# Attention scores of two mixers as stacked float32r products, a short run of ones at the beginning, and single waits for the embedding's banks

## What is computed

```
# sink mixer: 16 query heads, 4 key heads of width 64, window 128
scores = einsum('bnqkgd,bnskd->bnkgqs', q, kb) * 64 ** -0.5
scores = where(band, scores, -inf); m = max(scores, sink); e = exp(scores - m)
probs = e / (sum(e) + exp(sink - m)); out = probs @ v
# sparse mixer, 8 query heads, 2 key heads of width 64; N_CMP = 15 compressed keys
s_c = q @ k_cmp.T * scale ; s_s = q @ k_selected.T * scale ; s_w = q @ k_window.T * scale
o = g0 * softmax(s_c) @ v_cmp + g1 * softmax(s_s) @ v_slc + g2 * softmax(s_w) @ v_win
```

## Time and profile before

| | |
|---|---|
| median of 3 runs | 1202.47 us |
| the profiled execution | 1201.95 us, of which its span (first to last instruction) 1200.2 us |
| TensorE matmul (PE) busy | 1185.6 us, 99% |
| VectorE (DVE) busy | 747.8 us, 62% |
| ScalarE (ACT) busy | 619.5 us, 52% |
| GpSimd (POOL) busy | 43.9 us, 4% |
| DMA | 210.78 MB, 176 GB/s over the span |

### The profile page before, as it was taken

The page is one execution under the profiler, slowest core; times in us unless marked ns, Lnnn a source line. Parts: engine busy times, 40 slices in busy tenths (PEclk is TensorE's granted clock), DMA queues, the critical chain, the costliest instruction groups (busy, mean ns, idle before and its releaser), DMA issues.

```text
span 1200.2 us, 16205 instructions
## 1 busy us (share of the span) xinstructions
PE 1185.6 (99%) x6405; PEld 1006.8 (84%) x6405; DVE 747.8 (62%) x991; ACT 619.5 (52%) x925; POOL 43.9 (4%) x64
## 2 busy tenths in 40 slices
PE   9999999999999999999999999999999999999998
PEld 7888899898787889999888888888878788888887
DVE  6769645556865774554697455447986465554447
ACT  5464544344465544444456434436886674444445
POOL 2000000000000000000000000001111010000001
PEclk9999999999999999999999999999999999999999
DMA  8656554654653366556545565554651336555550
GB/s 285 216 186 209 193 191 163 209 196 154 228 177 114 114 210 197 190 177 204 181 146 183 198 206 179 180 172 144 191 167 69 114 124 210 198 188 175 176 175 36
DMA packets 119963, 210.78 MB, mean 176 GB/s; under 512 B 8320, under 2 KB 67024, under 8 KB 119888
## 3 DMA queue, kind: packets, MB, share of 16 engines
q1 hardware_dynamic: 119344, 209.35, 52.5%
q10 hardware_dynamic: 544, 0.40, 0.1%
HBM read 208.68 MB, written 1.05 MB: 175 GB/s over the span
## 4 chain that ended last, share of the span: by engine, by line
PE 91%; DVE 4%; ACT 2%; DMA 1%; issue 1%; POOL 0%; SPq 0%; ACTq 0%; DVEq 0%; POOLq 0%
PE psum L341 23%; PE psum L343 23%; PE psum L342 23%; PE psum L349 4%; PE psum L350 4%; PE psum L355 4%; PE psum L1430 2%; PE psum L1398 2%; DMA ring<-in_a_w_in 1%; DVE wl L324 1%; PE psum L1417 1%; PE psum L852 1%; PE psum L540 1%; PE psum L1404 0%; DVE arena L3607 0%
## 5 line engine op out<-in xcount | busy, mean ns | idle before, releaser
L293 DVE TENSOR_TENSOR wl<-ring,wh 128x2048 fp32r<-128x2048 f32 x131 | 300.0, 2292 | 263.1 <-ACT wh L284 263.0
L284 ACT ACTIVATE wh<-ring 128x2048 fp32r<-128x2048 f32 x131 | 250.6, 1915 | 215.2 <-PE psum L343 215.2
L341 PE MATMUL psum<-wh,xT_high 128*128 128x512 f32 (+4 forms) x592 | 231.4, 391 | 0.2 <-DVE wl L324 0.2
L343 PE MATMUL psum<-wh,xT_low 128*128 128x512 f32 (+4 forms) x592 | 225.1, 380 | 0.0
L342 PE MATMUL psum<-wl,xT_high 128*128 128x512 f32 (+4 forms) x592 | 224.4, 379 | 0.0
L341 PE MATMUL psum<-wh,hidT_high 128*128 128x512 f32 (+2 forms) x472 | 178.8, 380 | 0.2
L342 PE MATMUL psum<-wl,hidT_high 128*128 128x512 f32 (+2 forms) x472 | 178.0, 379 | 0.0
L343 PE MATMUL psum<-wh,hidT_low 128*128 128x512 f32 (+2 forms) x472 | 177.9, 378 | 0.0
L341 PEld LDWEIGHTS psum<-wh,xT_high 128*128 128x128 f32 x592 | 111.3, 188 | 21.6 <-issue 2.0
L343 PEld LDWEIGHTS psum<-wh,xT_low 128*128 128x128 f32 x592 | 111.2, 188 | 21.1
L324 DVE TENSOR_TENSOR wl<-ring,wh 128x1024 fp32r<-128x1024 f32 (+4 forms) x101 | 121.2, 1218 | 11.5 <-ACT wh L314 10.8
(11 more groups left out here) (323 smaller groups left out, 1479.6 us busy)
## 6 DMA issues: line engine op xcount, KB each, us to landing
ring<-in_mlp_w_up SPq DMA_DIRECT2D x32, 1024.0 KB, 5.5
ring<-in_mlp_w_down SPq DMA_DIRECT2D x32, 1024.0 KB, 5.0
ring<-in_ffn_wg SPq DMA_DIRECT2D x44, 512.0 KB, 4.0
ring<-in_ffn_wu SPq DMA_DIRECT2D x44, 512.0 KB, 5.0
ring<-in_ffn_wd SPq DMA_DIRECT2D x22, 1024.0 KB, 5.0
ring<-in_ple_w_gate SPq DMA_DIRECT2D x12, 1024.0 KB, 5.0
ring<-in_w_in SPq DMA_DIRECT2D x10, 1024.0 KB, 5.2
ring<-in_a_w_in SPq DMA_DIRECT2D x8, 1024.0 KB, 10.5
```

Source lines behind the costliest of these rows:

```text
L284: K.nc.scalar.activation(parts_of(K, n)[0][:, 0:w], K.ring[:, n % SLOTS, 0:w], ACT.Copy).then_inc(K.high_ready, 2)
L293: K.nc.vector.tensor_tensor(low[:, 0:w], K.ring[:, n % SLOTS, 0:w], high[:, 0:w].bitcast(F32), ALU.subtract).then_inc(K.low_ready, 2)
L341: nc.tensor.matmul(out, x[0], w[0], start=start, stop=False)
L343: return nc.tensor.matmul(out, x[1], w[0], start=False, stop=stop)
```

## The change

It has five parts.

1. In the sink mixer and in the selected, window and compressed units, queries and keys are split into high and low. For each head a query tile is stacked: its high part on the head's own 64 partitions and its low part on the other 64 (keys are there on both halves). One float32r matmul with the keys' high part then gives high by high and low by high, a second one with the keys' low part the rest. So a unit has four float32r matmuls of `size` columns and two masks in place of one float32 matmul of 2 x `size` columns and one mask. Compressed keys get 16 columns in place of 15. Forgetting attention stays as it was.
2. ScalarE writes the high parts (two activations over 64 partitions for a query tile pair, one for a key tile pair), VectorE the low parts (two and one), and TensorE waits for VectorE's counter `tile_dve`.
3. Before "lead" TensorE waits for the first of the embedding's banks alone, and before the two "turn" steps of the second half for the third and the fourth.
4. At the beginning TensorE runs five float32 matmuls of ones, 128 columns each, after the first turned pair of x; "bias" waits for its own two loads (`bias_loaded`), and `neg_sinks` is computed later; GpSimd's two selections and cast for `sel16` wait for "bias". Two masks move into other memory.
5. The lists of steps of both mixers are in a new order. In the sparse one TensorE's steps from the last query tile to the first scores are now `tiles 1`, `dense 2, 1, 1`, `cw1 1, 0, range(4)` and `scores 0`; in the sink mixer `tiles 0`, `tiles 2`, half of `dense 1, 0, 1`, `tiles 1`, the other half, `dense 1, 1, 0`, `scores 0`.

```diff
+        if u["halves"] is not None:
+            for a, (q, (high, low)) in enumerate(u["halves"]):
+                at = a * SEQ
+                wide = K.psum[:, self.banks[i], at:at + high.shape[1]]
+                nc.tensor.matmul(wide, q, high, start=True, stop=False)
+                nc.tensor.matmul(wide, q, low, start=False, stop=False)
+                lo, mask = u["mask"]
+                w = mask.shape[1]
+                mm = nc.tensor.matmul(out[:, a, lo:lo + w], K.ident16[:, :], mask, start=False, stop=True)
+            mm.then_inc(K.scores_ready.sem, 1)
+            return
...
                 if tile < 8:
-                    m = nc.scalar.activation(K.attT1[:, tile:tile + 2, :], src, ACT.Copy, scale=scale)
+                    for a, rows in enumerate((slice(0, HD), slice(HD, P))):
+                        m = nc.scalar.activation(K.attT1[a][rows, tile:tile + 2, :], src[rows, :, :], ACT.Copy,
+                                                 scale=scale)
                 else:
-                    for half in range(2):
-                        m = nc.scalar.activation(K.keys1[:, tile - 8:tile - 6, half, :], src, ACT.Copy,
-                                                 scale=K.half_rows[:, half:half + 1])
+                    m = nc.scalar.activation(K.keys1[0][:, tile - 8:tile - 6, :], src, ACT.Copy)
...
+            elif step == "tiles":
+                i, = args
+                tile, _ = TILES[i]
+                dve.wait_ge(K.tile_act.sem, tile_act0 + i + 1)
+                src = K.psum[:, TILE1_BANK[i], :].rearrange("p (j n) -> p j n", j=2)
+                if tile < 8:
+                    for a, rows, others in ((0, slice(0, HD), slice(HD, P)), (1, slice(HD, P), slice(0, HD))):
+                        m = nc.vector.scalar_tensor_tensor(K.attT1[a][others, tile:tile + 2, :], src[rows, :, :], scale,
+                                                           K.attT1[a][rows, tile:tile + 2, :].bitcast(F32), ALU.mult,
+                                                           ALU.subtract)
+                else:
+                    high, low = [k[:, tile - 8:tile - 6, :] for k in K.keys1]
+                    m = nc.vector.tensor_tensor(low, src, high.bitcast(F32), ALU.subtract)
+                m.then_inc(K.tile_dve.sem, 1)
...
             elif step == "scores":
                 i, = args
-                pe.wait_ge(K.tile_act.sem, tile_act0 + (3, 4, 5, 6)[i // 4])
+                pe.wait_ge(K.tile_dve.sem, tile_dve0 + (3, 4, 5, 6)[i // 4])
...
             elif step == "free" and embedding:
-                pe.wait_ge(K.act_took.sem, emb_took0 + 2 * TT)
+                i, = args
+                pe.wait_ge(K.act_took.sem, emb_took0 + i + 1)
...
+                if pair == 0:
+                    for i in range(5):
+                        nc.tensor.matmul(K.psum[:, 0, 0:P], K.ones[:, 0:P], K.ones[:, 0:P], start=True, stop=True)
...
             elif step == "bias":
-                dve.wait_ge(K.small_loaded, 16 * K.small_loads)
-                nc.vector.tensor_scalar(K.neg_sinks[:, :], K.sinks[:, :], -1.0, None, ALU.mult)
+                dve.wait_ge(K.bias_loaded, 16 * 2)
...
+        pool.wait_ge(K.gates_v.sem, 1)
         for part in (1, 2):
             select(2, K.sel[:, :, :], K.sel[:, :, :], [[-1, FOX], [0, P]], -32 * part, 1, 1.0, ALU.not_equal)
```

More of the change, by code:

```diff
@@ L1680, in sink_mixer @@
                 kv = pair // 2
-                units.append(dict(q=K.attT1[:, pair, t * P:(t + 1) * P], k=K.keys1[:, kv, :, 0:size], size=size, bias=None,
+                keys = [k[:, kv, 0:size] for k in K.keys1]
+                units.append(dict(halves=[(q[:, pair, t * P:(t + 1) * P], keys) for q in K.attT1], size=size,
                                   keep=None, sink=2 * pair,
@@ L1777, in steps @@
+        yield "values", 5
+        yield "take", 2, 1
         yield "turn", 6
-        yield "take", 2, 1
-        yield "dense", 2, 1, 1, range(2, 4)
+        yield "high", 8, 0
+        yield "rotate", 2
+        yield "out", 0, 0, 0
+        yield "shares", 1
+        yield "tiles", 4
         yield "turn", 7
-        yield "values", 5
         yield "values", 6
-        yield "out", 0, 0, 0
-        yield "high", 8, 0
+        yield "out", 0, 0, 1
         yield "values", 7
-        yield "rotate", 2
@@ L2154, in nsa_mixer @@
                 first_key, vc = (0, VSL) if kind == "slc" else (2, VWN)
-                u.update(k=K.keys2[:, first_key + kv, :, 0:size], v=[values(vc + kv * HD)] * 2)
+                keys = [k[:, first_key + kv, 0:size] for k in K.keys2]
+                u.update(halves=[(q[:, pair, q0:q1], keys) for q in K.attT2], v=[values(vc + kv * HD)] * 2)
             units.append(u)
@@ L2374, in steps @@
-        yield "scores", 13
-        yield "turn", 11
-        yield "scores", 14
-        yield "keep", 12
-        yield "dense", 4, 1, 1, range(2)
-        yield "keep", 13
-        yield "low", 16, 1
-        yield "values", 10
+        yield "shares", 2
+        yield "values", 9
+        yield "keep", 11
+        yield "values", 10
+        yield "turn", 11
+        yield "high", 16, 1
+        yield "scores", 13
+        yield "scores", 14
+        yield "dense", 4, 1, 1, range(2)
+        yield "keep", 12
@@ L2405, in steps @@
+        yield "keep", 16
+        yield "values", 14
+        yield "keep", 17
         yield "scores", 17
[L2406 removed]
+        yield "turn", 16
+        yield "low", 17, 1
+        yield "scores", 18
+        yield "dense", 5, 0, 1, range(2)
         yield "shares", 3
[L2408 to L2411 removed]
+        yield "values", 15
         yield "turn", 17
         yield "scores", 19
[L2414 removed]
@@ L2430, in steps @@
-        yield "scores", 21
-        yield "values", 17
-        yield "root2", 0, 0
-        yield "dense", 5, 1, 0, range(2, 4)
+        yield "turn", 18
+        yield "dense", 5, 1, 0, range(2)
+        yield "scores", 21
+        yield "values", 16
+        yield "root2", 0, 0
+        yield "mean", 4
+        yield "dense", 5, 1, 0, range(2, 4)
+        yield "scores", 22
+        yield "high", 18, 1
+        yield "low", 18, 0
+        yield "low", 18, 1
+        yield "shares", 4
+        yield "turn", 19
@@ L2434, in steps @@
+        yield "dense", 5, 1, 1, range(2)
+        yield "values", 17
+        yield "keep", 20
+        yield "dense", 5, 1, 1, range(2, 4)
+        yield "take", 5, 0
+        yield "take", 5, 1
+        yield "norm", 4
+        yield "high", 19, 0
         yield "keep", 21
-        yield "low", 18, 0
-        yield "turn", 19
-        yield "scores", 22
+        yield "zturn", 0, 0
         yield "values", 18
-        yield "norm", 4
-        yield "shares", 4
-        yield "take", 5, 0
-        yield "dense", 5, 1, 1, range(2)
@@ L2443, in steps @@
-        yield "low", 18, 1
-        yield "take", 5, 1
-        yield "high", 19, 0
-        yield "dense", 5, 1, 1, range(2, 4)
+        yield "values", 19
+        yield "tiles", 4
         yield "turn", 20
-        yield "zturn", 0, 0
+        yield "keep", 22
+        yield "high", 19, 1
         yield "group", 4
-        yield "tiles", 4
-        yield "high", 19, 1
-        yield "low", 19, 0
-        yield "values", 19
         yield "turn", 21
         yield "tiles", 5
+        yield "low", 19, 0
```

520 lines of the change are left out of this document (264 added, 256 removed).

## The result

The changed kernel takes 1204.71 us (median of 22 runs, 1203.48 to 1205.25), the kernel before 1202.57 us beside it (22 runs, 1201.4 to 1204.25). The ratio is 1.0013, with a 95% interval of 1.0007 to 1.0019: slower by 0.13%, less than the 0.2% that I had set as the bound for a change. The prediction was 1198.5 us with a range to 1201.8, and faster; it was wrong. The profiled execution took 1203.57 us, its span 1201.9. Of the 22 runs, 6 lie between 1203.5 and 1203.8 us at a mean granted clock of 1.000, 16 between 1204.4 and 1205.3 at 0.998 or 0.999. That difference turns out to be part of the answer.

A forecast was written before the change was run, and what follows sets the result against it. PE, busy 1185.6 of 1200.2 us, was taken as the bound. Units -4.8, banks -0.2, beginning -0.4, sparse waits +1.1 and sink wait +0.3 gave -4.0: from 1202.47 to 1198.5 us, range 1194.3 to 1201.8.

The forecast's parts named there:

- the sum on PE: TensorE work in both mixers' units: -3.0 sink 256-key, -2.6 selected and window 256-key, -1.4 128-key, +2.2 compressed; -4.8 us.
- less 0.05 of the first, which hides in part behind what is ahead: 128-key units: four loads of 0.11 and two of 0.03 make 0.50, less 0.05 for the first load: 0.45 us.
- every float32r matmul at 0.12, 0.59: Upper bound for a 128-key unit, each float32r matmul priced as with 256 columns: 0.59 us, 0.8 us lost.
- The load's price: Units with few columns: each load of a query tile's 128 stationary columns takes 0.11 us on TensorE.
- the literal reading of "Weight-path perf modes": Small units: float32r loads fast, units only stream, sum near -8.8 us; rival with loads hidden and no wait 1193.1, chance 0.12.
- 0.6 us at first scores, 1.1 in all: Sparse mixer: TensorE waits 0.6 us for low parts at first scores, 1.1 with first values and scores 4; bounds 0 and 4.1.
- DVE the bound in the sparse mixer: Rival: DVE's whole new 4.1 us there shows on PE, +3.0 net; 1201.2 us in all, chance 0.20.
- a wait of 0.3 at the first scores: Sink mixer: 4.4 us until the low parts against 4.2 us of cover; a wait of 0.3, bounds 0 and 1.2.
- DVE is idle for 12.2 of 40 us: Sink mixer, 340 to 380 us: this idle time was to hide DVE's 6.9 us of new work.
- Banks: Tails, ahead of "lead": waiting for embedding's banks singly starts it about 0.85 us earlier, 0.2 kept; -0.2 together, bounds 0 and -1.3.
- in the two others I found the same: Two other tails with an embedding: x comes when PE has done what stands ahead of it; all three together -0.2 us.
- The beginning: "bias" freed from waiting for head gains brings forward gates, scan and a low half: -0.4 us, bounds -0.6 and +0.7; ones cost nothing.

The follow-up runs named there:

- small edits: Kernel before plus ones at the beginning, embedding's banks waited for singly, gate bias and GpSimd's selections waited for apart, both mixers as before: 1200.91 us, 0.9981.
- filling: Changed kernel plus 18 bf16 matmuls that nothing reads in the sparse mixer's two waits: 1203.16 us, 1.0005; same in the kernel with one mask for both heads: 1201.04.
- the new lists alone: Kernel before, float32 scores kept, with both mixers' step lists of the changed kernel: 1205.65 us, 1.0026.
- the doubled and the moved work: Changed kernel with query tiles' low parts computed twice on VectorE (sparse 1208.35 us, sink 1209.58); with second sparse query tile's split moved behind first scores, cw1 cover added (1205.41).
- banks alone: Kernel before with only the embedding's banks waited for singly: 1201.61 us, 0.9992.

## Why the prediction was wrong

The account: before 1202.55; small edits to 1200.91; sink stage +0.34 and sparse stage +1.95 from the table; clock +1.2 to 1.5 at the median (filling gave 1.55). That makes 1204.4 to 1204.7, against 1204.71. Cut the other way: the new lists alone +3.1, the small edits -1.6, the new scores in the new lists -0.7, the clock +1.2, which makes 1204.6. The -0.7 is the two stages against those of the old scores with the new lists, -1.98 (0.07 of it the banks') and +1.19.

- **The step that failed is the sum on PE, -4.8 us.** By the table the rest went from 117.84 to 117.05 and from 149.25 to 149.32, -0.72. The units themselves gave nothing. Below is the mean price of each kind, start to start without idle time, with what the matmul behind a unit has over the usual pitch of its shape (0.23 for 512 columns, 0.11 for a turn):

| 8 units each | forecast | measured | forecast, us | measured, us |
|---|---|---|---|---|
| sink, 256 keys | 1.08 to 0.70 | 1.08 to 0.77 | -3.0 | -2.5 |
| sink, 128 keys | 0.54 to 0.45 | 0.54 to 0.67 | -0.7 | +1.0 |
| selected, window, 256 | 0.97 to 0.64 | 1.01 to 0.77 | -2.6 | -1.9 |
| selected, window, 128 | 0.54 to 0.45 | 0.58 to 0.65 | -0.7 | +0.6 |
| compressed | 0.16 to 0.44 | 0.22 to 0.55 | +2.2 | +2.6 |

  Most of the miss, 3.0 us, is the 128-key units, which lost what they should have gained. The reason is in the step "less 0.05 of the first, which hides in part behind what is ahead": nothing hides behind a mask of 0.04, the matmul behind one pays 0.14 to 0.15, and the one behind the unit pays too. Four matmuls at 0.11, two masks at 0.04 and two exposures of 0.03 to 0.04 make the 0.59 from start to start. That is the upper bound that I had set aside ("every float32r matmul at 0.12, 0.59"), and with the matmul behind it the unit is above the bound. The old price of 1.08 was right: where such a unit of the kernel before ends after 0.89 us, the dense matmul behind it has 0.42 in place of 0.23 (351.40 to 351.81). The units' sum is -0.1 and the stages' -0.72, because the new lists also move the price of other rows: the 24 turned tiles of the sink mixer take 2.9 us in place of 2.3, the turned probabilities of the sparse one 0.8 less.
- **The new lists stood at nothing.** The sum has no term for the order of steps; the prediction only said that it might remove waits. With the old scores the lists cost 3.1 us: 2.25 in the sink stage, half of it idle time and half PE's rows, and 0.84 in the sparse one. They are needed all the same, since the new scores cost 10.5 us more without them.
- **The load's price was right.** 0.11 for a query tile's load, at 128 and at 16 columns (902.83 to 902.94). The Trainium skill, "TensorE: Matmul & The Clock Gate", section "LDWEIGHTS (loading the stationary operand)", gives 107 ns for 128 columns, and the runs agree; the literal reading of "Weight-path perf modes", by which these loads would be fast, does not fit 0.11 us for a matmul of 16 columns.
- **The waits in the sparse mixer: the first right in place and cause, the second not seen.** "0.6 us at first scores, 1.1 in all" was 1.14 at the scores, by the low parts, as foreseen: with most of one low part left out it is gone. The 1.45 at the first turn is not DVE's: it is there with the old scores in the new lists, and 1.53 with less work on DVE. It belongs to the lists, in which the turn comes right behind the scores. The rival "DVE the bound in the sparse mixer" (0.20) is near in part: the stage's idle time grew by 1.88, under its bound of 4.1, but 0.99 us of such growth come with the lists alone. What holds of it is that DVE has no room there, as the doubled and the moved work show.
- **The clock was missing from that term.** I looked for it only at the beginning. The two waits cost another 1.2 to 1.5 us through it at the median. An execution in which the clock stays up has only their length, as the profiled one. With the old scores in the new lists, where only the second wait stands, 6 of 7 executions have a mean clock of 1.000.
- **The sink mixer hides the change's own low parts, and no more.** The forecast had a wait of 0.3 at the first scores; it is 0.06. New gaps of 0.40 at 341, 0.19 and 0.40 at 382 us are 1.0 of the 1.13 us of new idle time, and they are those of the new lists. But "DVE is idle for 12.2 of 40 us" is an average: of 6.0 us of further work 3.6 show.
- **Banks: -0.2 forecast, -0.9 measured.** The reading of the first tail was right in kind (0.10 kept there, forecast 0.2), that "in the two others I found the same" was wrong: 0.35 and 0.44 are kept in the second and third (33.23 to 32.88, and 6.75 to 6.31 us, from first to last transpose, banks alone).
- **The beginning: -0.4 forecast, -0.7 measured.** At 111 us the profiled executions with the new waits stand between 0.4 us ahead of before and 0.1 behind, so part of the 0.7 is the slow end that is gone (1203.25 us with the banks alone, 1201.26 with all). That it was the clock between 5 and 20 us rests on one profile, that of the old scores with the new lists; in no profile was it seen beside a run that differs in nothing else, so this stays open. The ones cost nothing, as said.
- **What was right:** DVE's +11 us, the gap before "lead" and the wait for x behind it. That the time came out within 0.2% of before has no merit: +3.1 for the lists, -1.6 for the small edits and a price of the units near nothing happen to cancel.

## What to carry to other kernels

A product split over heads is paid in loads where it has few columns: count the loads, and add what the matmul behind a group pays, since it doesn't show in the group's own rows. One mask for two heads in place of two gave 2.3 us here. A new order of steps is an edit like any other: run it without the rest before putting a gap down to the rest. Work added to an engine with a third of its time free is not hidden when it stands in front of a step that TensorE needs; double it in a trial and see. Waits such as these two are to be priced with the clock behind them, and a few unread matmuls in them tell how much that is. When a bundle of edits is slower, run the small ones alone: here they were the gain.

## What was not expected of the hardware

- The clock granted fell to 0.50 right behind 2.6 us of waits with 0.55 us of work between them, and was back within about 3 us; 16 of 22 executions of the changed kernel have the longer time and the lower mean clock that go with it. With the waits filled by matmuls that nothing reads, the two profiles show 1.00 there, and all 20 times lie in or below the lower group of their base. The Trainium skill, "TensorE: Matmul & The Clock Gate", section "HAM oscillation — how this bites in real kernels", describes such losses for waits on DMA; here it is waits for VectorE and ScalarE.
- A bf16 matmul's start comes 0.04 us before that of the float32r one behind it, which then has 0.14 to 0.20 to its successor where 0.11 to 0.12 is usual; a dense one of 512 columns has 0.32 behind a mask of 128 or 256 columns and 0.42 behind one of 512, where 0.23 is usual. What a mask costs is seen in the row behind it.
- The beginning's clock is not the same in every profile: 0.83 between 5 and 12 us with the old scores and the new lists, 1.00 in the kernel before, and nothing that differs between the two runs so early.
